# Three products of rounded parts in place of one float32 product, in the output projections of attention and of the recurrences

## The reference, cut to what matters

```python
o_a = mla_branch(...)              # attention output, 1024 x 512
o_b = rwkv7_branch(...)            # two recurrences, normed and gated, 1024 x 512
y_a = o_a @ w_o_l[:MLA_WIDTH]      # 512 x 1024 weights
y_b = o_b @ w_o_l[MLA_WIDTH:]      # 512 x 1024 weights
gates = jax.nn.sigmoid(gate_cols.reshape(B, S, N_BRANCHES, D) + b_gate[l])
x = x + (gates[:, :, 0] * y_a + gates[:, :, 1] * y_b) @ w_merge[l]
```

## Time and profile before

| | |
|---|---|
| median of 3 runs | 3272.03 us (3270.03 to 3272.25) |
| the profiled execution's own time | 3276.29 us |
| its span, first to last instruction | 3274.5 us |
| TensorE busy | 3153.8 us, 96% of the span |
| VectorE, ScalarE, GpSimd busy | 64%, 40%, 27% |
| mean granted clock of TensorE | 0.988 of 2.4 GHz |

### The profile page before, as it was taken

How to read it: one execution, slowest core, us unless ns; L and a number is a source line. 1 busy time by engine, 2 the same in 40 slices (tenths; PEclk the granted TensorE clock), 3 DMA queues, 4 the chain that set the end, 5 groups by cost and what they waited for, 6 DMA issues and landing times.

```text
span 3274.5 us, 61761 instructions
## 1 busy us (share of the span) xinstructions
PE 3153.8 (96%) x26560; PEld 2540.2 (78%) x26560; DVE 2084.6 (64%) x3031; ACT 1297.0 (40%) x2289; POOL 887.3 (27%) x778
## 2 busy tenths in 40 slices
PE   8999999999999988999999999999999999999998
PEld 8678776778887776467888888878677878888887
DVE  5263465666776665847899877762455575565686
ACT  4333334555555432124333344443333343333444
POOL 1232233222322222100576740000000025566100
PEclk9999999999999999999999999999999999999999
DMA  4251245112211121532123247522102322322753
GB/s 151 68 155 49 71 161 178 42 41 64 71 54 46 66 94 44 209 131 91 71 105 117 97 154 247 165 95 89 36 32 74 132 87 85 120 101 97 264 160 116
DMA packets 128016, 346.46 MB, mean 106 GB/s; under 512 B 15792, under 2 KB 19520, under 8 KB 124928
## 3 DMA queue, kind: packets, MB, share of 16 engines
q1 hardware_dynamic: 106592, 258.09, 23.7%
q0 software_dynamic: 21152, 84.42, 6.9%
HBM read 246.51 MB, written 95.94 MB: 105 GB/s over the span
## 4 chain that ended last, share of the span: by engine, by line
PE 83%; DVE 9%; ACT 4%; issue 2%; DMA 1%; POOL 0%; SPq 0%; DVEq 0%; ACTq 0%; POOLq 0%
PE ps L369 42%; PE ps L368 39%; PE ps L372 3%; DVE X L378 2%; DVE AR L378 2%; DVE SM L389 1%; DVE W L378 1%; DVE WS L378 1%; ACT HT L1240 1%; ACT AR L375 1%; DVE EX L378 0%; ACT WS L375 0%; ACT W L2219 0%; DMA AR<-rw_d 0%; DVE HT L382 0%
## 5 line engine op out<-in xcount | busy, mean ns | idle before, releaser
L378 DVE TENSOR_TENSOR WS<-W,WS 128x512 fp32r<-128x512 f32 (+1 forms) x284 | 341.4, 1203 | 251.1 <-ACT WS L375 250.9
L368 PE MATMUL ps<-HH,WS 128*128 128x512 f32 x1280 | 394.1, 389 | 0.0
L368 PE MATMUL ps<-TO,WS 128*128 128x512 f32 x1440 | 345.9, 389 | 0.0
L375 ACT ACTIVATE WS<-W 128x512 fp32r<-128x512 f32 (+1 forms) x284 | 210.0, 740 | 315.2 <-PE ps L369 170.9
L368 PEld LDWEIGHTS ps<-TO,WS 128*128 128x128 f32 x1440 | 270.3, 188 | 56.1
L368 PEld LDWEIGHTS ps<-HH,WS 128*128 128x128 f32 x1280 | 240.2, 188 | 49.9
L368 PE MATMUL ps<-HL,WS 128*128 128x512 f32 x640 | 249.0, 389 | 0.0
L368 PE MATMUL ps<-TO 128*128 128x512 f32 x936 | 226.8, 390 | 0.2 <-DVE TO L378 0.2
L369 PE MATMUL ps<-AR 64*64 64x64 f32 (+2 forms) x5440 | 204.1, 242 | 21.4 <-ACT AR L375 9.6
L368 PE MATMUL ps<-WS 128*128 128x512 f32 x888 | 215.1, 390 | 0.1
L375 ACT ACTIVATE X<-ps 128x512 f32<-128x512 f32 (+1 forms) x168 | 100.5, 598 | 284.5 <-PE ps L369 128.6
(11 more groups left out here) (367 smaller groups left out, 6409.2 us busy)
## 6 DMA issues: line engine op xcount, KB each, us to landing
AR_b<-h_d SPq DMA_DIRECT2D x154, 256.0 KB, 2.9
AR<-rw_d SPq DMA_DIRECT2D x104, 256.0 KB, 4.1
W<-in_w_fg SPq DMA_DIRECT2D x44, 512.0 KB, 3.8
W<-in_w_fu SPq DMA_DIRECT2D x44, 512.0 KB, 4.9
h_d<-FST POOLq DMA_DIRECT2D x20, 1024.0 KB, 4.4
x_d<-X POOLq DMA_DIRECT2D x24, 512.0 KB, 4.6
W<-in_w_tok SPq DMA_DIRECT2D x24, 512.0 KB, 4.0
rw_d<-X POOLq DMA_DIRECT2D x40, 256.0 KB, 3.3
```

The source lines that it names most:

```text
L368: return pe.e.matmul(o, l, r, start=start, stop=stop, skip_group_check=True)
L375: return e.e.activation(o, x, ACT.Copy)
L378: return e.e.tensor_tensor(o, x, y, op)
```

## The change

1. The product `outa` and the product `outb` are each made from three float32r products. A group is 12 `mm` in place of 4.
2. The operands of `outa` are split in the scans. When the attention is over, ScalarE copies the 8 pieces (128 x 512) of `OAT3` and GpSimd subtracts, one piece for each turn of `scans` (`att_out_ae`, `att_out_ge`). The first copy waits for the load of `OAT3`.
3. The first four tiles of `w_o` and the first four gates lie elsewhere (`AR`, memory of scan 0), so SyncE loads them when scan 0 has ended on all engines, and no longer behind the attention. They are split one a turn (`wo_first_*`). Tiles 4 to 7 are split in the group norm (`wo_hi` in `gn_ae`, `wo_lo` in `gn_ge`).
4. In the group norm ScalarE copies a tile's transposes twice (high part and whole), and GpSimd subtracts (`ob_lo`) two tiles later. The second product's weights are split by ScalarE behind tiles 0 and 7 of `TORD` and by GpSimd behind its last bonus (`wb_lo`).
5. The rounded parts take the place of x in memory, so x is loaded again (`x_again`) only when outb is over, behind the merge weights 1 to 4 and ahead of those from 5 on.

```diff
+        XF = region(room, "XF", 8192, FR)
...
+        OBL1 = region(room, "OBL1", 2048, FR)
+        region(room, "AR_f", 8192 + 2048)
+        OBL0 = region(room, "OBL0", 2048, FR)
...
-        GT = [HT[:, 4096 + 512 * i:4608 + 512 * i] for i in range(4)]
-        WO = [HT[:, 6144 + 512 * i:6656 + 512 * i] for i in range(4)]
-        OAT3 = v3(HT[:, 0:4096], 4)
+        GT = [AR[:, 10240 + 512 * i:10752 + 512 * i] for i in range(4)]
+        WO = [AR[:, 8192 + 512 * i:8704 + 512 * i] for i in range(4)]
+        WOL = [WS[:, 512 * i:512 * i + 512] for i in range(4)]
+        WOH = [HL[:, 4096 + 512 * i:4608 + 512 * i] for i in range(4)]
+        OAT3, OAL3, OAH3 = v3(HT[:, 0:4096], 4), v3(HH[:, 0:4096], 4), v3(HH[:, 4096:8192], 4)
         OF = [X[:, 0:4096], X[:, 4096:8192]]
         VV = AR[:, 0:4096]
         SQT = AR[:, 6144:8192]
         BON, ACC = [SQT[:, 0:512], SQT[:, 1536:2048]], [SQT[:, 512:1024], SQT[:, 1024:1536]]
-        OBT = [EX[:, 2048:3072], EX[:, 3072:4096], AR[:, 12288:13312], AR[:, 13312:14336]]
+        OBR, OBL = (EX[:, 2048:4096], AR[:, 12288:14336]), (OBL0, OBL1)
+        OBH = (XF[:, 0:2048], XF[:, 2048:4096])
         TORD = (3, 4, 2, 5, 1, 6, 0, 7)
+        WBH = [XF[:, 4096 + 512 * t:4608 + 512 * t] for t in TORD]
+        WBR, WBL = [[z[:, 512 * n:512 * n + 512] for n in range(8)] for z in (W, WL)]
...
+        def att_out_sp(sp):
...
+        def att_out_ae(ae):
+            for k in range(4):
+                for h in range(2):
+                    ae.wait_ge(*at("dma_oat", 0))
+                    cp(ae, OAH3[:, k, half(h)], OAT3[:, k, half(h)]).then_inc(*ae.sig("ae_mix", "oh", k, h))
+                    yield
+
+        def att_out_ge(ge):
+            for k in range(4):
+                for h in range(2):
+                    ge.wait_ge(*at("ae_mix", "oh", k, h))
+                    tt(ge, OAL3[:, k, half(h)], OAT3[:, k, half(h)], OAH3[:, k, half(h)].bitcast(F32),
+                       ALU.subtract).then_inc(*ge.sig("ge_mix", "ol", k, h))
+                    yield
+
+        def wo_first_sp(sp):
+            for g in ("pe", "ve", "ae", "ge"):
+                sp.wait_ge(*end("scan0", g))
             for n in range(4):
-                load(n)
+                outa_load(sp, n)
             for i in range(4):
-                gate(i)
+                outa_gate(sp, i)
             yield
+
+        def wo_hi(ae, n):
+            ae.wait_ge(*at(f"dma_wo{n % 4}", n))
+            if n >= 4:
+                ae.wait_ge(*at("pe_mix", "a", 2 * (n - 4) + 1))
+            cp(ae, WOH[n % 4], WO[n % 4]).then_inc(*ae.sig("ae_mix", "wh", n))
+
+        def wo_lo(ge, n):
+            ge.wait_ge(*at("ae_mix", "wh", n))
+            tt(ge, WOL[n % 4], WO[n % 4], WOH[n % 4].bitcast(F32), ALU.subtract).then_inc(*ge.sig("ge_mix", "wl", n))
+
+        def wo_first_ae(ae):
+            for n in range(4):
+                yield
+                wo_hi(ae, n)
+
+        def wo_first_ge(ge):
+            for n in range(4):
+                yield
+                wo_lo(ge, n)
+
...
         def outa_pe(pe):
-            yield
             for n in range(8):
-                w3 = v3(WO[n % 4], 4)
+                wh, wl = v3(WOH[n % 4], 4), v3(WOL[n % 4], 4)
                 for h in range(2):
                     b = take(pe, "outa", n, h)
-                    pe.wait_ge(*at(f"dma_wo{n % 4}", n))
-                    pe.wait_ge(*at("dma_oat", 0))
+                    pe.wait_ge(*at("ge_mix", "wl", n))
+                    pe.wait_ge(*at("ge_mix", "ol", 3, 1))
                     for k in range(4):
-                        x = mm(pe, ps[:, b, :], w3[:, k, :], OAT3[:, k, half(h)], k == 0, k == 3)
+                        mm(pe, ps[:, b, :], wh[:, k, :], OAH3[:, k, half(h)], k == 0, False)
+                        mm(pe, ps[:, b, :], wh[:, k, :], OAL3[:, k, half(h)], False, False)
+                        x = mm(pe, ps[:, b, :], wl[:, k, :], OAH3[:, k, half(h)], False, k == 3)
                     x.then_inc(*pe.sig("pe_mix", "a", 2 * n + h))
...
-        def scans(e, scan, att, outa):
-
-            def att_and_loads():
+        def scans(e, scan, att, after_att, after_first):
+
+            def first_scan():
+                yield from scan(e, 0)
+                e.close("scan0", e.name)
+                yield from after_first(e)
+
+            def att_then():
                 yield from att(e)
                 e.close("att", e.name)
-                next(outa)
-
-            s0, s1, at_ = scan(e, 0), scan(e, 1), att_and_loads()
+                yield from after_att(e)
+
+            s0, s1, at_ = first_scan(), scan(e, 1), att_then()
             for _ in range(7):
                 next(s0)
                 next(at_)
             interleave(s0, s1, at_)
...
         def gn_ae(ae):
             stored(ae, 0)
-            for t in TORD:
-                yield
+            made = 0
+            for n, t in enumerate(TORD):
                 ae.wait_ge(*at("pe_mix", "gT", t))
-                for j in range(2):
-                    x = cp(ae, (EX[:, 2048:4096], AR[:, 12288:14336])[j].rearrange("p (a b) -> p a b", a=2)[:, :, t * P:(t + 1) * P],
-                           v3(ps[:, bank("gnT", t), 256 * j:256 * j + 256], 2))
-                    if j:
-                        x.then_inc(*ae.sig("ae_mix", "gT", t, frees=("gnT", t)))
-            yield
+                cp(ae, of_tile(OBH, t), ps[:, bank("gnT", t), :]).then_inc(*ae.sig("ae_mix", "gh", t))
+                cp(ae, of_tile(OBR, t), ps[:, bank("gnT", t), :]).then_inc(*ae.sig("ae_mix", "gT", t, frees=("gnT", t)))
+                if n < 4:
+                    wo_hi(ae, n + 4)
+                while made < (0, 0, 0, 0, 0, 0, 5, 8)[n]:
+                    ae.wait_ge(*at("dma_wob", 7))
+                    cp(ae, WBH[made], WBR[made]).then_inc(*ae.sig("ae_mix", "bh", made))
+                    made += 1
+
+        def ob_lo(ge, t):
+            ge.wait_ge(*at("ae_mix", "gT", t))
+            tt(ge, of_tile(OBL, t), of_tile(OBR, t), of_tile(OBH, t).bitcast(F32), ALU.subtract).then_inc(*ge.sig("ge_mix", "ob", t))
+
+        def wb_lo(ge, n):
+            ge.wait_ge(*at("ae_mix", "bh", n))
+            tt(ge, WBL[n], WBR[n], WBH[n].bitcast(F32), ALU.subtract).then_inc(*ge.sig("ge_mix", "bl", n))
 
         def gn_ge(ge):
             for n, t in enumerate(TORD):
@@ -2005,6 +2083,17 @@
                    ALU.mult).then_inc(*ge.sig("ge_mix", "bon0", t))
                 ge.wait_ge(*at("ge_mix", "bon0", t))
                 tt(ge, bon, bon, LB_, ALU.add).then_inc(*ge.sig("ge_mix", "bon", t))
+                if n >= 2:
+                    ob_lo(ge, TORD[n - 2])
+                if 1 <= n < 5:
+                    wo_lo(ge, n + 3)
+            wb_lo(ge, 0)
+            ob_lo(ge, TORD[6])
+            for n in range(1, 5):
+                wb_lo(ge, n)
+            ob_lo(ge, TORD[7])
+            for n in range(5, 8):
+                wb_lo(ge, n)
...
-                        for t in range(3):
-                            sp.e.dma_start(xt(t), a["x"][t * P:(t + 1) * P, :]).then_inc(*dma(f"dma_x{t}", "again"))
-                    if h == 0 and n >= 3:
-                        sp.e.dma_start(xt(n), a["x"][n * P:(n + 1) * P, :]).then_inc(*dma(f"dma_x{n}", "again"))
+
+        def x_again(sp):
+            sp.wait_ge(*at("pe_mix", "b", 1, 7))
+            for t in range(NT):
+                sp.e.dma_start(xt(t), a["x"][t * P:(t + 1) * P, :]).then_inc(*dma(f"dma_x{t}", "again"))
 
         def outb_pe(pe, gn):
             for h in range(2):
                 for n in range(8):
                     if h == 0 and n == 2:
                         next(gn)
-                    w3 = v3(W[:, 512 * n:512 * n + 512], 4)
+                    wh, wl, oh, ol = v3(WBH[n], 4), v3(WBL[n], 4), by_feature(OBH[h]), by_feature(OBL[h])
                     b = take(pe, "outb", h, n)
-                    pe.wait_ge(*at("dma_wob", 7))
+                    o = v3(ps[:, b, :], 4)
+                    pe.wait_ge(*at("ge_mix", "bl", n))
                     pe.wait_ge(*at("ae_mix", "gT", 7 if h else 0))
                     for k in range(4):
-                        x = mm(pe, ps[:, b, :], w3[:, k, :], OBT[k][:, half(h)], k == 0, k == 3)
+                        mm(pe, o, wh[:, k, :], oh[:, k], k == 0, False)
+                        mm(pe, o, wl[:, k, :], oh[:, k], False, False)
+                    pe.wait_ge(*at("ge_mix", "ob", 7 if h else 0))
+                    for k in range(4):
+                        x = mm(pe, o, wh[:, k, :], ol[:, k], False, k == 3)
                     x.then_inc(*pe.sig("pe_mix", "b", h, n))
...
-            weights_sp(sp, 1, first["1"])
+            weights_sp(sp, 1, 5)
+            x_again(sp)
+            weights_sp(sp, 5, first["1"])
```

More of the change, by code:

```diff
@@ L250, in program @@
         room.close()
+        room = ExitStack()
+        XF = region(room, "XF", 8192, FR)
+        room.close()
         X = region(ctx, "X", 8192)
@@ L281, in program @@
```

(53 more changed lines are left out.)

2 lines of the change are left out of this document (removed).

## The result

The changed kernel takes 3291.05 us (median of 4 runs, 3290.50 to 3297.36), the kernel before 3271.24 (4 runs). The ratio is 1.0065, 95% interval 1.0053 to 1.0077: 0.65% slower, some 20 us. The forecast was 3285, with 3262 to 3293 as its range: the sign is right and the time lies inside, but +12.7 us was forecast where +19.8 was measured.

What follows compares the result with a forecast made beforehand. TensorE was taken as the bound (83% of the chain), VectorE nearly a second in the group norm. 7.7 + 1.5 + 2.0 + 11.7 - 10.2 = +12.7 us on the median 3272.03 gave 3285 us, range 3262 to 3293.

Steps and rivals of the forecast that it cites:

- The wait for `OAT3`: Scans: ScalarE's first copy waits for the 2 MB load and delays scan 0's exponential: +7.7 us, bounds 0 and 9.
- the two: Scans: no longer queued `w_o` and gates (up to 3 us gained) against a new stretch at 1.2 GHz: 0 together.
- The other splits: Scans: seven more ScalarE copies and eight GpSimd subtractions, most falling into gaps: +1.5 us, at most 4.4.
- The end of scan 0: ScalarE's `wo_hi(0)` waits for the first `w_o` load ahead of scan 1's copy: +2.0 us, bounds 0 and 4.
- The group norm: GpSimd's subtractions and bonus operations shut out VectorE's two-input operations; six steps take 64.5 us, before 52.8: +11.7 us.
- rival A: Group norm: TensorE stays the bound, steps of 8.3 us; the part gains 3, total 3270; chance 0.2.
- outb: 16 groups of 2.72 us, 11.45 us less, part lost in the last tile: -10.2 us, bounds -11.4 and -6.
- The last tile: VectorE's last acc about 9.7 us behind the seventh in place of some 9; TensorE waits 0.9 for its transposes.
- x again: After outb: 4 MB of x loaded again before the merge needs it: 0, some 3 us if cover were gone.
- B: Scans: other engines have work enough or the load is much faster: sum +5.0, 3277; chance 0.12.
- C: Group norm: TensorE's clock falls behind its idle time, some 27 us more over six steps, 3311; chance 0.05.

Runs made afterwards that it cites:

- experiment 1: Changed kernel with the copies and subtractions of the attention's output begun 8 turns later, so the load of `OAT3` has landed: 3281.69 us, ratio 1.0034.
- experiment 7: Changed kernel with `OAT3` copies 8 turns later, first `w_o` tiles 2 turns later, merge weight 1 split early, VectorE's outb low one group later: 3275.04 us.
- experiment 10: Changed kernel with `OAT3` copies and first `w_o` tiles later, `ob_lo` on VectorE from PSUM, merge weight 1 split early, outb's low one group later: 3269.99 us.
- experiment 2: Changed kernel with the rounding of the first four `w_o` tiles begun 2 turns later behind the end of scan 0: 3286.90 us, ratio 1.0044.
- Experiment 3: Changed kernel without GpSimd's `ob_lo` and `wo_lo` subtractions in the group norm; TensorE reads the high parts in their place: 3283.05 us, ratio 1.0037.
- experiment 5: Changed kernel with merge weight 1 split within outb, behind group 6 of the second half: 3284.37 us, ratio 1.0041.
- experiment 6: Changed kernel with VectorE's low of outb taken one group later, the split of merge weight 1 left in place: 3284.48 us, ratio 1.0042.
- the repaired form: Only outb in parts, `outa` in float32; `ob_lo` on VectorE from PSUM, merge weight 1 split early, outb's low one group later: 3261.82 us, ratio 0.9975.

## Why the prediction was right, and where it was not

The sign was right, and so were the places and causes of the losses: +12.7 forecast, +19.8 measured by the medians, inside the range. The size was 7 us short. Two terms were off in the same direction and one in the other.

- **The wait for `OAT3`, +7.7.** The place, the cause and the queue were right, and the exponential is 7.7 to 7.8 us late in three runs (8.4 to 8.7 in the three whose loads took 8.8 to 9.05 us, the changed kernel's own among them). What was mis-sized is the clock behind it: "I take 0 for the two". The stretch at half clock that the prediction set against the old one was longer. Before, the low stretch was 0.55 for 3 us; after, 0.50 from 1140 to 1152, and TensorE had work for nearly 5 of these. The whole wait, with what follows it, is about 10 by experiment 1, above the prediction's bound of 9.
- **The other splits, +1.5**: 1.4 to 2.3 (experiments 1, 7 and 10). The eight copies take 5.0 us of ScalarE, so most of that fell into gaps.
- **The end of scan 0, +2.0**: 1.8, and experiment 2 takes away 2.45.
- **The group norm, +11.7**: 8.7 to 9.5. The written-out hand-over of the two engines can be read off the rows above one operation at a time, each within some 0.5 us of its place, and VectorE's mean for two-input operations is 1.11 us (40.1 us in 36) against 0.81 before. Step by step it was 11.78, 10.63, 9.53, 10.80, 9.38 and 9.41, against 12.2, three of 11.1 and two of 9.5. More than half of the difference is the third: there `wo_lo` (1350.02) started behind an operation of VectorE that already ran, and beside the next, on PSUM, so it held up only the one behind those, by 0.35 us (1.04 in place of 0.69). Experiment 3 shows that the loss is GpSimd's subtractions (8.7 to 9.5 less without them, TensorE's products kept), and rival A falls with it.
- **outb, -10.2**: this is the step that failed. It came to -2.5 (-4.6 and the last tile's +2.2), outside its bounds of -11.4 and -6. The prediction saw VectorE's round of 2.7 us, "no faster than TensorE's", and then said that "eight banks of PSUM and the 20 us until the second half of the merge needs it cover a lag". The banks did. But the next thing in VectorE's queue is not the merge's second half: it is the split of merge weight 1, written behind all 16 rounds. VectorE comes late out of the last tile and carries that lag, some 5 us, unshortened through its rounds (2.71 us each against TensorE's 2.79, but 4.20 for the one that also splits weight 0; the last starts at 1442.53, TensorE has left outb at 1436.96), and TensorE needs weight 1 only one weight later. 5.3 of the missing 7.7 us are this (experiment 5; 6.0 in experiment 6). The last tile costs 2.2 where 0.9 was priced, since its acc is 10.79 us behind the seventh and not 9.7: 1.3 more. It stays at 10.8 to 10.9 in every experiment with outb in parts. Its rows show four two-input operations of 1.07, 1.66, 1.67 and 1.68 us in place of 0.69, beside GpSimd's subtractions of the second product's weights (`wb_lo`, from 1388.82 on), which every experiment keeps; none was made without them. And the groups come 2.79 us apart, not 2.72: 1.0 over the 14 behind the last acc. The three make 7.6.
- **x again, 0**: right. Its 8 loads landed in 7.6 us (median), no wait names them, and the rest of the kernel is as long as before.

The rivals. A (TensorE stays the bound) is refuted by the step rows, B (the scans cover the load) by three microseconds without any engine busy. C happened in part: in the group norm TensorE's clock did fall behind its idle stretches, but VectorE was busy all along (3.86 us or more of each 4) and never waited for it, so it cost nothing. It is not free in itself: in experiment 3, where VectorE has less to do, TensorE's low stretch there makes VectorE wait 1.27 us. Two stretches of the changed kernel, TensorE's granted clock 0.50 and 0.64 beside a VectorE with 3.93 and 3.90 of 4 us:

```profile
1324.00:1328.00 4.00, 3.09 (x7) 1.92 (x8) 3.93 (x8) 1.60 (x3) 0.20 (x1) 0.50 0.37 97
...
1348.00:1352.00 4.00, 4.00 (x10) 2.08 (x9) 3.90 (x6) 1.60 (x3) 1.98 (x2) 0.64 0.73 206
```

Between the two profiles, the forecast's sum from t0 is 10.2 us too little (+5.8 in the scans, of which 3 to 4 belong to that one execution, +7.7 in outb, -3.0 in the group norm, the rest small), against a start that was 2 us earlier. That the result still lies in the range, 2 us below its upper end, is partly luck: that end adds the bounds of four terms and nothing for outb, which missed most, and the group norm, priced too high, made up 3 us of it.

Why splitting `outa` does not pay here: in outb the work is bound by TensorE and the repaired form gains 10.6 us there, less 2.2 in the last tile; in `outa` the step is bound by VectorE and by what GpSimd does beside it, so the shorter products free an engine that then waits.

## What to carry to other kernels

Cutting an engine's work pays only where the next engine has room in that very stage: give each stage its own balance (here 92% of VectorE beside a full TensorE) and change only the stage with room, as the version with outb alone did. When a lag between two engines is said to be covered, follow the lagging engine's queue to the first thing that someone else waits for, whatever stage it belongs to. A subtraction that reads SBUF on GpSimd is dear beside a busy VectorE; the same one on VectorE with an input still in PSUM cost 0.68 us and no one else's time.

## What was not expected of the hardware

- After 10.2 us without work (1136.99 to 1147.18) TensorE's granted clock stayed at 0.50 through the first 5 us of renewed work in small matmuls, and was 0.84 in the next 3. An exponential 7.7 to 8.4 us late went with 9.4 to 10.3 us at the end of scan 0. The Trainium skill, TensorE: Matmul & The Clock Gate, What's actually happening, has just these two levels and ties them to how busy TensorE has lately been; the rows agree as to the levels.
- Float32r products of outb start 0.2325 us apart (2.79 us for 12), those of `outa` and of the long stretch 0.228 and 0.2267. outb's moving operand lies in four blocks of 128 columns, the others' in one of 512; that this is the reason was not tested.
- GpSimd's operations are lengthened as well: 1.04 and 1.27 us where they started first, 1.49 and 1.62 in the step above, where an operation of VectorE had been waiting. The Trainium skill, SBUF — State Buffer, Who interferes with whom, says that who comes first blocks the other fully; both engines' rows agree.
- The start of the changed stages varied by 9 us between executions (t0 from 1124.3 to 1133.6) with no edit ahead of it, so single profiles can't be compared by their spans here.
